# Attention in units of eight heads: one set of score banks, turned probabilities in four banks

## The reference

```python
DILATED_PATTERNS = ((128, 1), (512, 4), (2048, 16))          # window, dilation; 8 heads of 64
# per dilation: tokens of one residue form a sequence; blocks of 128 queries see 256 keys
scores = einsum('nbqhd,nbkhd->nbhqk', qb, kb) * dh ** -0.5
scores = where(abs(key - query) <= 64 and key in range, scores, -1e30)
m = max(scores);  p = exp(scores - m);  den = sum(p)
o = einsum('nbhqk,nbkhd->nbqhd', p, vb) / den;  lse = m + log(den)
# the three dilations' o are then joined with softmax(lse) as weights
```

## Time and profile before

| | |
|---|---|
| profiled execution | 3449.12 us, its span 3447.3 us |
| runs | 3448.32, 3453.84, 3455.07 us |
| busy over the span | PE 95%, DVE 47%, ACT 41%, POOL 15% |
| chain that ended last | PE 48%, its lines all of the expert phase |
| attention phase | about 836 to 1278 us |
| PE, ACT, DVE busy in it | 429.1, 369.5, 315.1 of 442 us |

### The profile page before, as it was taken

The page is one execution under the profiler, slowest core; times in us unless marked ns, Lnnn a source line. Parts: engine busy times, 40 slices in busy tenths (PEclk is TensorE's granted clock), DMA queues, the critical chain, the costliest instruction groups (busy, mean ns, idle before and its releaser), DMA issues. The chain is left out here.

```text
span 3447.3 us, 56676 instructions
## 1 busy us (share of the span) xinstructions
PE 3265.6 (95%) x21950; PEld 2958.8 (86%) x21950; DVE 1633.2 (47%) x3584; ACT 1424.5 (41%) x3020; POOL 533.6 (15%) x483
## 2 busy tenths in 40 slices
PE   7999999997999978999379999999999999999997
PEld 4888888886777766888279999999999999999997
DVE  5445444543777765555643333333333333333454
ACT  4333333333888873333133333333333333333443
POOL 0111111112212113222011101111101111001232
PEclk9999999998999998999589999999999999999999
DMA  5111111114743444554245445555445555345685
GB/s 204 58 54 48 50 57 50 51 52 142 236 120 115 126 123 147 195 191 160 78 141 159 135 138 162 160 154 159 132 150 159 159 157 152 126 154 159 221 272 198
DMA packets 337566, 474.60 MB, mean 138 GB/s; under 512 B 22992, under 2 KB 250064, under 8 KB 337232
## 3 DMA queue, kind: packets, MB, share of 16 engines
q1 hardware_dynamic: 318784, 403.72, 35.8%
q0 software_dynamic: 18576, 68.03, 7.1%
HBM read 360.26 MB, written 111.41 MB: 137 GB/s over the span
## 5 line engine op out<-in xcount | busy, mean ns | idle before, releaser
L2002 DVE TENSOR_TENSOR warm_lo<-warm_stage,warm_hi 128x2048 fp32r<-128x2048 f32 x192 | 439.9, 2292 | 623.9 <-ACT warm_hi L1508 622.9
L1508 ACT ACTIVATE warm_hi<-warm_stage 128x2048 fp32r<-128x2048 f32 x192 | 366.5, 1909 | 4.3 <-DMA warm_stage<-in_w_gate 3.2
L2108 PE MATMUL exp_ps_g<-exp_xT_hi,warm_lo 128*128 128x384 f32 x1024 | 345.9, 338 | 1.7 <-DVE exp_xT_lo L2009 1.7
L2108 PE MATMUL exp_ps_g<-exp_xT_lo,warm_hi 128*128 128x384 f32 x1024 | 345.9, 338 | 0.0
L2108 PE MATMUL exp_ps_u<-exp_xT_lo,warm_hi 128*128 128x384 f32 x1024 | 345.9, 338 | 0.0
L2108 PE MATMUL exp_ps_u<-exp_xT_hi,warm_lo 128*128 128x384 f32 x1024 | 345.9, 338 | 0.0
L2108 PE MATMUL exp_ps_g<-exp_xT_hi,warm_hi 128*128 128x384 f32 x1024 | 345.9, 338 | 0.0
L2108 PE MATMUL exp_ps_u<-exp_xT_hi,warm_hi 128*128 128x384 f32 x1024 | 345.9, 338 | 0.0
L995 ACT ACTIVATE att_prob<-att_prob,att_o 128x256 f32<-128x256 f32 (+1 forms) x576 | 265.7, 464 | 71.7 <-DVE att_o L1039 68.5
L1886 POOL DMA_INDIRECT scratch_y<-exp_ye,route_slots x45 | 98.4, 2187 | 1190.2 <-ACT exp_ye L1976 1180.8
L1960 ACT ACTIVATE exp_hT_hi<-exp_hid 128x768 fp32r<-128x768 f32 x64 | 54.2, 847 | 428.0 <-DVE exp_hid L2023 428.0
(11 more groups left out here) (313 smaller groups left out, 7769.6 us busy)
## 6 DMA issues: line engine op xcount, KB each, us to landing
warm_stage<-in_w_gate SPq DMA_DIRECT2D x128, 512.0 KB, 4.4
warm_stage<-in_w_up SPq DMA_DIRECT2D x128, 512.0 KB, 4.5
warm_stage<-in_w_down SPq DMA_DIRECT2D x128, 512.0 KB, 4.4
mix_o<-scratch_o SPq DMA_DIRECT2D x72, 264.0 KB, 3.0
att_v<-scratch_v SPq DMA_DIRECT2D x64, 256.0 KB, 3.9
scratch_xn<-mix_xn SPq DMA_DIRECT2D x24, 520.0 KB, 3.5
memory_x<-in_x SPq DMA_DIRECT2D x24, 512.0 KB, 3.3
att_v<-scratch_v SPq DMA_DIRECT2D x192, 64.0 KB, 2.0
```

The lines of the kernel that those rows point to most:

```text
L1508: self.nc.scalar.activation(self.hi[:, m % self.RW, :, :], self.stage[:, m % self.RS, :, :], ACT.Copy).then_inc(self.hi_sb, 1)
L2002: nc.vector.tensor_tensor(w_lo[:, m % RW, :, :], stage[:, m % RS, :, :], w_hi[:, m % RW, :, :].bitcast(F32), ALU.subtract).then_inc(s["w_l ...
L2108: x_ = nc.tensor.matmul(ps[:, f, 0:S], a[:, m % RW, k, f * P:(f + 1) * P], b[:, k, :], start=(n == 0), stop=(n == 3 * KC - 1))
```

## The change

A unit becomes a whole block of eight heads. Its scores fill all four banks of `ps_s` in two positions of two pairs; which pairs come first alternates from block to block (`pair_of`). The scores of block c+2 wait for all masks of block c+1 (first position) and for the copy of the turned output of block c (second position). `ps_p` has four banks, one for each pair. `ps_o` is gone: the values' product goes into a bank of `ps_s` that the masks of block c+1 have already left (`turned_out`), and the turn back goes into the fourth bank of `ps_p`. To make room in SBUF, `o` has three buffers (from four), the gathered queries three (from four), `prob` two blocks (from three half blocks), `oT` one (from two), and two half-width masks share one of now seven entries.

PE's order for block c becomes: four `turn`, four `values`, `scores` of block c+2, `back` of block c. ACT and DVE do the next block's exponentials and masks between their copies.

```diff
-    AHEAD = 2
-    RV, RO, RP, RQ, RS = 4, 4, 3, 4, 4
+    RV, RO, RP, RQ, RS = 4, 3, 2, 3, 4
+    def pair_of(c, i):
+        return 2 * ((c + i // 2) % 2) + i % 2
-        masks = ph.sb("masks", [P, 8, 2 * P])
+        masks = ph.sb("masks", [P, 7, 2 * P])
-        prob = ph.sb("prob", [P, RP, 2, 2, 2 * P])
-        probT = ph.sb("probT", [P, 2, 4, P])
+        prob = ph.sb("prob", [P, RP, 4, 2, 2 * P])
+        probT = ph.sb("probT", [P, 4, 4, P])
-        oT = ph.sb("oT", [P, 2, 4, P])
+        oT = ph.sb("oT", [P, 4, P])
         ps_s = ph.psum("ps_s", [P, 2, 2, 2, 2 * P])
-        ps_p = ph.psum("ps_p", [P, 2, 4, P])
-        ps_o = ph.psum("ps_o", [P, 2, D_A])
+        ps_p = ph.psum("ps_p", [P, 4, 4, P])
+        def turned_out(c):
+            return ps_s[:, (c + 1) % 2, 0, :, :].rearrange("p j (h q) -> p (j h) q", h=2)
 # PE
-                def scores(n):
+                def scores(c):
-                    ge(pe, masked, 2 * (n - 1))
+                    for pos in range(2):
+                        if pos == 0:
+                            ge(pe, masked, 4 * c)
+                        else:
+                            ge(pe, oT_sb, c - 1)
+                        for jj in range(2):
+                            for f in range(2):
+                                j = pair_of(c, 2 * pos + jj)
+                                x_ = nc.tensor.matmul(ps_s[:, j // 2, f, jj, 0:b.W], ...)
+                        x_.then_inc(scored, 1)
+                def turn(c, i):
+                    pe.wait_ge(p_sb, 4 * c + i + 1)
+                    ge(pe, pT_b if i % 2 else pT_a, 2 * c - 1 + i // 2)
+                    if i == 3:
+                        ge(pe, o_sb, c)
...
+                def values(c, i):
+                    pe.wait_ge(pT_b if i % 2 else pT_a, 2 * c + i // 2 + 1)
+                    if i == 0:
+                        pe.wait_ge(v_loaded[c % RV], v_count[c])
+                        if c + 1 < NB:
+                            pe.wait_ge(masked, 4 * (c + 1) + 2)
...
-                for n in range(NU):
-                    turn(n, 0)
-                    turn(n, 1)
-                    if n % 2 and n > 1:
-                        back(n // 2 - 1)
-                    if n + AHEAD < NU:
-                        scores(n + AHEAD)
-                    values(n, 0)
-                    values(n, 1)
+                for c in range(NB):
+                    for i in range(4):
+                        turn(c, i)
+                    for i in range(4):
+                        values(c, i)
+                    if c + 2 < NB:
+                        scores(c + 2)
+                    back(c)
 # ACT
+                for c in range(NB):
+                    more = c + 1 < NB
+                    if more:
+                        exps(c + 1, 0)
+                    out_p(c, 0)
+                    if more:
+                        exp(c + 1, 1, 0)
+                    out_p(c, 1)
+                    if more:
+                        exp(c + 1, 1, 1).then_inc(p_sb, 1)
+                        exps(c + 1, 2)
+                    out_oT(c)
+                    if more:
+                        exps(c + 1, 3)
 # DVE
+                        if i == 0 and c >= RO:
+                            dve.wait_ge(o_stored[c % RO], o_count[c - RO])
...
+                for c in range(NB):
+                    more = c + 1 < NB
+                    if more:
+                        mask(c + 1, 0)
+                        mask(c + 1, 1)
+                    if c:
+                        out_o(c - 1)
+                    out_p(c, 0)
+                    if more:
+                        mask(c + 1, 2)
+                    out_p(c, 1)
+                    if more:
+                        mask(c + 1, 3)
```

More of the change, by code:

```diff
@@ L717, in __init__ @@
         edge = 0 if at == 0 else 2 if last else 1
-        self.mask = 6 + seq if dil == 16 else 3 * self.which + edge
+        self.mask = (6, seq * P) if dil == 16 else (3 * self.which + edge, 0)
         self.reach = min(SEQS[seq], P * at + 192) if dil == 1 else SEQS[seq]
@@ L930, in scores @@
                         seen[0] = need
-                    if half == 0:
-                        pe.wait_ge(q_set if c else first_q, max(c, 1))
-                    ge(pe, masked, 2 * (n - 1))
[L934 to L944, removed]
+                    pe.wait_ge(q_set if c else first_q, max(c, 1))
+                    for pos in range(2):
[6 more added lines that the diff above has]
+                                j = pair_of(c, 2 * pos + jj)
+                                x_ = nc.tensor.matmul(ps_s[:, j // 2, f, jj, 0:b.W], q[f * HD:(f + 1) * HD, c % RQ, j, :], b.keys(kP, f, j),
+                                                      start=True, stop=True)
+                        x_.then_inc(scored, 1)
@@ L945, in turn @@
+                def turn(c, i):
+                    b = blocks[c]
+                    pe.wait_ge(p_sb, 4 * c + i + 1)
+                    ge(pe, pT_b if i % 2 else pT_a, 2 * c - 1 + i // 2)
+                    if i == 3:
+                        ge(pe, o_sb, c)
                     for f in range(2):
                         for k in range(b.chunks):
[L947 removed]
+                            x_ = nc.tensor.transpose(ps_p[:, i, b.chunks * f + k, :], prob[:, c % RP, i, f, k * P:(k + 1) * P], ident[:])
@@ L948, in turn @@
                     x_.then_inc(pT_ps, 1)
-                def values(n, jj):
-                    c, half = n // 2, n % 2
+                def values(c, i):
                     b = blocks[c]
-                    pe.wait_ge(pT_b if jj else pT_a, n + 1)
-                    if half == 0 and jj == 0:
+                    j = pair_of(c, i)
+                    pe.wait_ge(pT_b if i % 2 else pT_a, 2 * c + i // 2 + 1)
+                    if i == 0:
                         pe.wait_ge(v_loaded[c % RV], v_count[c])
-                        ge(pe, o_sb, c - 1)
+                        if c + 1 < NB:
+                            pe.wait_ge(masked, 4 * (c + 1) + 2)
@@ L957, in values @@
                     for k in range(b.chunks):
                         for f in range(2):
[L959 to L962, removed]
+                            x_ = nc.tensor.matmul(turned_out(c)[f * HD:(f + 1) * HD, j, :], v[:, c % RV, k, (2 * j + f) * HD:(2 * j + f + 1) * HD],
+                                                  probT[:, i, b.chunks * f + k, :], start=(k == 0), stop=(k == b.chunks - 1))
@@ L966, in back @@
                     pe.wait_ge(oT_sb, c + 1)
+                    pe.wait_ge(pT_b, 2 * c + 2)
                     for j in range(4):
-                        x_ = nc.tensor.transpose(ps_o[:, c % 2, j * P:(j + 1) * P], oT[:, c % 2, j, :], ident[:])
+                        x_ = nc.tensor.transpose(ps_p[:, 3, j, :], oT[:, j, :], ident[:])
                     x_.then_inc(back_ps, 1)
                 pe.wait_ge(padded, 4)
-                for n in range(AHEAD):
-                    scores(n)
+                scores(0)
@@ L974, in _ @@
+                scores(1)
                 pe.wait_ge(consts, 32)
-                for n in range(NU):
-                    turn(n, 0)
-                    turn(n, 1)
-                    if n % 2 and n > 1:
-                        back(n // 2 - 1)
-                    if n + AHEAD < NU:
-                        scores(n + AHEAD)
-                    values(n, 0)
-                    values(n, 1)
-                back(NB - 1)
+                for c in range(NB):
[6 more added lines that the diff above has]
+                    back(c)
@@ L986, in _, with exp @@
             @block.scalar
             def _(act):
-                def exps(n, jj):
-                    c, half = n // 2, n % 2
+                def exp(c, i, f):
                     b = blocks[c]
[L991 to L997, removed]
+                    h = D_A + 2 * pair_of(c, i) + f
+                    if f == 0:
+                        act.wait_ge(masked, 4 * c + i + 1)
+                    p = prob[:, c % RP, i, f, 0:b.W]
+                    return nc.scalar.activation(p, p, ACT.Exp, bias=o[:, c % RO, h:h + 1], scale=-1.0,
+                                                accum_out=o[:, c % RO, HA + h:HA + h + 1])
@@ L999, in out_oT, with exps, out_p @@
+                def exps(c, i):
+                    exp(c, i, 0)
+                    exp(c, i, 1).then_inc(p_sb, 1)
+                def out_p(c, pos):
+                    b = blocks[c]
+                    act.wait_ge(pT_ps, 4 * c + 2 * pos + 1)
+                    ge(act, pv_ps, 4 * (c - 1) + 2 * pos + 1)
+                    nc.scalar.activation(probT[:, 2 * pos, 0:2 * b.chunks, :], ps_p[:, 2 * pos, 0:2 * b.chunks, :], ACT.Copy).then_inc(pT_a, 1)
                 def out_oT(c):
                     act.wait_ge(pv_ps, 4 * (c + 1))
-                    ge(act, back_ps, c - 1)
@@ L1002, in out_oT @@
[L1002 to L1008, removed]
+                    ge(act, back_ps, c)
```

(39 more changed lines are left out.)

4 lines of the change are left out of this document (1 added, 3 removed).

## The result

The changed kernel is slower: 3458.93 us, median of 20 runs (3453.06 to 3464.27), against 3449.91 for the kernel before, again 20 runs, in the same sessions. Ratio 1.0028, 95% interval 1.0021 to 1.0035. Forecast was 11 us faster; measured is 9 us slower. The profiled execution has a span of 3453.9 us.

What follows compares the result with a forecast made beforehand. PE was taken to bound wide blocks, ACT narrow ones. Wide -22, narrow -5, start +8.4, weights +6.2 sum to -12 us, taken as -11: median 3443 (profiled 3438), range 3425 to 3461.

Steps and rivals of the forecast that it cites:

- fewer switches: PE's order in a block: three changes of tile shape instead of six, gaps about 0.19 us each, PE's floor 6.1 us.
- the loop through DVE: Wide blocks: scores wait for DVE's masks of the block before; round 6.2 us instead of 6.66, 22 us gained over 48 blocks.
- two masks 0.69 with about 0.1 for reading out and handing over: End of DVE's round in a wide block: last two masks and the hand-over to the next scores, ending at 6.15 us.
- the start and the weights: Waits for stores with three output buffers: 8.4 us lost at the attention stage's start, 6.2 net at the output weights' load.
- The usual landing, 3.0 us, fits. Two places don't.: Three output buffers: 4.1 us may pass before a mask needs a store; only the start and the output weights' load exceed it.
- The 16 narrow blocks: First 16 blocks of dilation 16: ACT's 4.21 us is the floor, 4.25 taken, 0.3 gained each, 5 us in all.
- about 4.55, as now: Last eight narrow blocks, two stores each: DVE's round through copy, stores, landing and masks takes about 4.55 us, no gain.
- The DVE round is longer: Rival, 24%: DVE's round 6.45 us; wide blocks gain 10, narrow 2, stalls cost 15: +3 us, 3457, no change.
- The store sets the pace for good: Rival, 11%: at dilation 4 the store's round makes 24 wide blocks 7.1 us instead of 6.2: +11 us, 3465, slower.
- No stall: Rival, 14%: stores land in 3 us or masks have slack, so the whole 27 to 31 us is gained: 3425.
- gaps belong to waits: Rival, 4%: PE's gaps come with waits, not tile shapes; nothing saved, stalls stay: +12 to +15 us, 3468.

## Why the prediction was wrong

**Right: fewer switches.** Three gaps instead of six, no instruction more, and the shape as their cause; the run with the turn back between the scores shows it. The gaps aren't 0.19 each: they are 0.17 and 0.33 (0.33 stands already in the row at 905.01 of the earlier trace rows, where I worked with about 0.22), the three left come to 0.67 once no wait is in them, and PE's floor is the 6.16 of the run with the third mask ahead, not 6.1.

**Right in kind, too small in size: the loop through DVE.** The round was named step by step and the 6.32 us are its time, as the third mask ahead shows. I had 6.15 to 6.2. The transposes' side fits (3.46 forecast from scores to first copy, 3.52 measured, 973.52 to 977.04); the mis-sized term is the end: "two masks 0.69 with about 0.1 for reading out and handing over", 0.79 us. Measured from the mask's start at 978.95 to the next scores at 979.84 it is 0.89: the last mask runs its full 0.42, not the 0.345 at which a next one starts, and 0.12 pass from the end of its read-out to the scores. With the first copy 0.06 later the round is 6.32 for the 6.2 taken: 0.12 us x 48 is 6 of the 20 us between forecast and result.

**Right: the start and the weights.** The first blocks were to lose 8.4 us. Four buffers lose 5.3 there (rounds of 6.68, 8.10, 9.73 and 6.05 us against 6.32), and the stores of block 5 lie 4.0 us further back again with three, counted from PE's first scores: 9.3. The weights were to cost 6.2 us net: the three rounds take 30.30 us, 11.3 over their 18.96, less the 4.0 of before: 7.4. The cause was right at both places, and together it is 2 us off. The share of three buffers in it is 4.0 at the start and 8.8 at the weights (30.30 against 21.52 in the run with four). So close a fit at the start is in part luck: there the run with four buffers and spread weights loses 2.7 us by the same count, with the same program up to that point, where the one with four buffers lost 5.3.

**Wrong: "The usual landing, 3.0 us, fits. Two places don't."** This is the step that failed. I held a median against the room, and for narrow blocks did not work the room out at all for the first 16, but counted a gain of 0.3 us each. They had landings of 2.0 to 2.4 with a single 3.7, and four buffers hid that one. In the new narrow round the mask that needs a store comes 2.4 us after the store's issue (1095.98 to 1098.37). Each slow one, 3.2 to 4.2 us, stops DVE, and with it the copies that PE and ACT wait for. The 16 narrow blocks lost 2 us instead of gaining 5. For the last eight, with two stores each, the room was worked out, but as just enough, "about 4.55, as now": their first five rounds take 26.61 us (1248.84 to 1275.45) instead of 22.81, 3.8 lost instead of nothing. Together that is 11 us of the 20. The run with four buffers in the same order brings it back (70.97 us for the 16 rounds that took 76.87), and 4.32 against the 4.25 forecast shows that the narrow round itself was sized well.

**The rivals.** "The DVE round is longer" came nearest in size, 3457 against 3458.9, by luck: its round of 6.45 was 6.32, and what it had too much there the narrow blocks lost. "The store sets the pace for good" was right in sign and in kind (3465), but at another place: I put it at dilation 4, where SP issues twelve DMAs a block, and it came at dilation 16, where the round is shortest, at the slow stores and in the last eight blocks. At dilation 4 rounds are 6.39 instead of 6.32 (stores 16 to 29, 83.02 us in 13 rounds), by that 1.6 us for its 24 blocks. "No stall" and "gaps belong to waits" are refuted. A gain of 18 us was there, and 27 us were given back for one buffer of 2 KB per partition.

## What to carry to other kernels

When a shorter round and a smaller ring of buffers come together, hold the room of each wait against the slowest landings of the transfers behind it, not their median: the old ring's depth hides them in the old trace. Where products of several tile shapes alternate on PE, order by shape: two switches more cost 0.35 us a block here. And where small stores are awaited with little room, a large load in their queue belongs in pieces: that was worth 10 us with three buffers, and about 3 with four, which the runs don't tell from nothing.

## What the runs showed of the hardware that was not expected

Stores land later beside instruction packets. Of 46 stores of the 2048 tokens' narrow blocks (16 in the changed kernel, 15 before, 15 with four buffers), 21 had no packet of queues 8 or 14 within some 3 us after their issue, and all 21 landed in 2.0 to 2.1 us; the 25 with one took 2.1 to 4.6. That is seen side by side, not tried: no run moved or removed these packets. Which engine's code they bring, and why some of them cost nothing, stays open.
